# Adding each token's two expert rows on TensorE instead of on ScalarE and VectorE

## The chip, the cores and the metric

The kernel runs on one core of one Trainium2 chip. The metric is the device time of one execution in microseconds (us), the median of several runs. Five engines have instruction streams of their own: TensorE (PE), VectorE (DVE), ScalarE (ACT), GpSimd (POOL) and SyncE (SP, which here only waits and issues transfers). They meet through semaphores, which are called by their names in the code (`y_back`, `over_sum`, `x_done`).

## The reference

One step of a two-layer backbone, for 128 context tokens and 256 latent tokens (384 in all, width 1024, float32). Layer 0 has a Hyena and grouped-query attention mixer, layer 1 multi-head latent attention (MLA). Both layers end in a mixture of experts, and only its end matters here:

```python
    scores = sigmoid(x @ router_w)                   # 16 experts, the best group, the best two in it
    wsel = wsel / sum(wsel)                          # two gates for each token
    mid = silu(a) * up * gates[:, :, None]
    y = einsum('tef,efd->td', mid, w_down)           # each token: gate0 * row of expert 0 + gate1 * row of expert 1
    ...
    h = _rmsnorm(x, norm_ffn[l]) * (1.0 + sc2) + sh2
    x = x + g2 * _moe(h, ...)                        # g2: a vector over the 1024 columns, one for each group of tokens
```

After layer 0 the next layer begins with a norm of x; after layer 1 x is the output.

## The kernel before

The 384 tokens stand in three tiles (t = 0, 1, 2) of 128 partitions; `x[:, t, :]` is the residual stream. An expert stage (`experts(l)` on every engine, called from `moe(l)`) gathers token rows, runs the 16 experts in blocks of 64 rows on TensorE, and scatters each block's rows, not yet gated, into a DRAM table `y_rows` of 768 rows: row i is token i's first choice, row 384 + i its second. Rows that don't fit into an expert's 64 places go into further "over" blocks, in a loop on all engines (`over_block`). The last over block isn't scattered: TensorE adds its rows straight to their tokens with a table of zeros and gates (`token_table`).

What stands behind the loop in each layer is called the tail here:

- SP (`rows_back`, L770 to 776) and ACT (L1909 to 1912) wait for the last scatter (`over_stored`) and read `y_rows` back, tile by tile: ACT the first choices into `y_of[0]` (which is `xn`), SP the second choices into `y_of[1]`. Each transfer is 128 rows of 4 KB, one to a partition (512 KB). Both count on `y_back[t]`; a tile has landed when it stands at 32 more than before.
- ACT multiplies a tile's first rows by their gates (`scale_first`, L1915 to 1917).
- DVE multiplies the last over block by the vector g2 (L2595 to 2596, table `gate_halves`), PE turns it into token rows with `token_table` (L1393 to 1397, six products of 64 rows) in two PSUM banks for each tile, and counts `over_sum`.
- DVE joins a tile in `join(l, t, part)`: part 0 adds the second rows times their gates (L2605), part 1 multiplies by g2 (L2607), part 2 adds the result to x (L2609) and then the two PSUM banks (L2614), and counts `x_done`.

After layer 0, ACT and DVE norm each tile (`next_norm`, `norm_mean`, `norm_scale`) between the joins. PE runs 14 products on constants, which nobody reads, then `mixer_turn(1, 0)` (transposes of tile 0), ACT and nobody else modulates the transposed tile 0 (eight instructions of L1774), and PE projects it (`latent_in(0)`). ACT's order is: norm of tile 0, norm of tile 1, modulation of tile 0, norm of tile 2. SP waits for all of `y_back` before it sends the weights of `latent_in`, and for `over_sum` of all tiles before it sends the MLA projection weights; POOL waits for `over_sum` of all tiles before it loads nine small tables of MLA (`in_mla`). After layer 1, SP stores each tile of x when it is done (L824), and the program ends.

The order of every engine's work is that in which the code is written.

Of the kernel before, what the change touches and what calls it, by code (L numbers as in the profile page):

```python
# [193 lines left out]
def build_step(nc, d, o):  # L194
# [180 lines left out]
    with ExitStack() as ctx:  # L375
# [42 lines left out]
        gates_read = ck[:, 96:96 + 2 * NT].rearrange("p (t m) -> p t m", m=2)  # L418
# [120 lines left out]
        y_of = [xn, view(7680, NT, D)]  # L539
# [6 lines left out]
        gate_halves, token_ids, token_table = view(5120, 2, HY), view(6464, T), view(6848, T)  # L546
# [62 lines left out]
        y_scaled = sem("y_scaled")  # L609
# [84 lines left out]
        def _(sp):  # L694
# [134 lines left out]
        def _(pool):  # L829
# [45 lines left out]
            for l in range(2):  # L875
# [60 lines left out]
                pool.wait_ge(over_stored[l], nb * 16)  # L936
                pool.tensor_tensor(pool_mark[:, 2:3], pool_mark[:, 3:4], pool_mark[:, 3:4], ALU.mult)
# [36 lines left out]
        def _(pe):  # L974
# [254 lines left out]
            def experts(l):  # L1229
# [412 lines left out]
            for _ in range(14):  # L1642
# [69 lines left out]
        def _(act):  # L1712
# [133 lines left out]
            def experts(l):  # L1846
# [64 lines left out]
                for t in range(NT):  # L1911
                    act.dma_start(y_of[0][:, t, :], y_rows[P * t:P * t + P, :]).then_inc(y_back[t], 16)
                act.wait_ge(over_gathered[l], nb * 16 + 32)
# [127 lines left out]
            scale_first(0, 0)  # L2041
            scale_first(0, 1)
            next_norm(0)
            scale_first(0, 2)
# [45 lines left out]
            for t in range(NT):  # L2090
                scale_first(1, t)
# [3 lines left out]
        def _(dve):  # L2095
# [411 lines left out]
            def over_lists(l):  # L2507
# [4 lines left out]
                dve.tensor_copy(place_gate[:, :, 1], ps[MT_BANKS[0]][:, 256 + 2 * NOVER:256 + 3 * NOVER])  # L2512
                dve.drain().then_inc(over_rows, 1)
                dve.tensor_copy(row_now[:, :], rows_over[:, 1:2]).then_inc(row_ready[l], 1)

            def over_scales(l):
# [5 lines left out]
                for half in range(2):  # L2522
                    rows = slice(HALF * half, HALF * half + HALF)
                    dve.tensor_copy(gate_halves[rows, :, :], gb[rows, :, HY * half:HY * half + HY])

            def experts(l):
# [68 lines left out]
                for g in range(2):  # L2595
                    ins = dve.tensor_tensor(ysb[:, 1, HY * g:HY * g + HY], ps[Y_BANKS[0]][:, :], gate_halves[:, g, :], ALU.mult)
                ins.then_inc(over_done[l], 1)

            def join(l, t, part):
                ya, yb = y_of[0][:, t, :], y_of[1][:, t, :]  # L2600
                settle()
                if part == 0:
                    dve.wait_ge(y_back[t], 32 * (l + 1))
                    dve.wait_ge(y_scaled, NT * l + t + 1)
                    dve.scalar_tensor_tensor(out=ya, in0=yb, scalar=gates_read[:, t, 1:2], in1=ya, op0=ALU.mult, op1=ALU.add)  # L2605
                elif part == 1:
                    dve.tensor_tensor(ya, ya, gb[:, GRP[t], :], ALU.mult)  # L2607
                else:
                    dve.tensor_tensor(x[:, t, :], x[:, t, :], ya, ALU.add)  # L2609
                    dve.wait_ge(over_sum, NT * l + t + 1)  # L2610
                    settle()
                    for half in range(2):
                        part_of = x[:, t, HY * half:HY * half + HY]
                        ins = dve.tensor_tensor(part_of, part_of, ps[SUM_BANKS[t][half]][:, :], ALU.add)  # L2614
                    ins.then_inc(x_done, 1)
# [207 lines left out]
            for part in range(3):  # L2823
# [5 lines left out]
            join(0, 1, 2)  # L2829
# [4 lines left out]
            join(0, 2, 2)  # L2834
# [29 lines left out]
            for t in range(NT):  # L2864
                for part in range(3):
# [21 lines left out]
```

## Time and profile before

| | us |
|---|---|
| median of 3 runs | 871.5 (865.86 to 874.1) |
| the profiled execution, its own time | 869.39 |
| its span, first to last instruction | 867.5 |
| PE busy | 789.1 (91%) |
| DVE busy | 374.6 (43%) |
| ACT busy | 283.6 (33%) |
| POOL busy | 107.2 (12%) |
| HBM traffic over the span | 269 GB/s |
| mean granted TensorE clock | 0.968 of full |

How to read it: PE is busy nearly everywhere, and the chain that ended last runs 58% of the span through PE. The places where PE stands idle are the first microseconds and the two tails, after 457 us and after 844 us of the span. Busy shares over the whole span say nothing on a tail; for that the timeline of the tail is read, row by row. In the rows below, "x12" is the number of instructions in a row (a float32 product is shown as two), a bracket is the idle time of the engine ahead of the row and what ended it, PEld is the weight load, and SPq, ACTq are instructions that issue a transfer.

### The profile page before, as it was taken

What the parts mean: (1) busy time and instruction counts of PE and PEld (TensorE: products, weight loads), DVE (VectorE), ACT (ScalarE), POOL (GpSimd) and SP (SyncE); (2) the same over time, 40 slices, a digit from 0 to 9 for tenths busy, and PEclk for the clock granted to TensorE, in tenths of its full rate; (3) what the DMA queues carried; (4) which work ended last, traced back from release to release, by engine and by line L of the source; (5) the groups of instructions that cost most, each with busy time, mean ns of one, the idle gap of its engine ahead of it and who ended that gap; (6) DMA issues with size and microseconds to landing.
All of it is one profiled execution on the core that took longest, in us unless ns stands there. A gap on an engine that the chain in (4) does not pass through costs nothing.

```text
span 867.5 us, 12012 instructions
## 1 busy us (share of the span) xinstructions
PE 789.1 (91%) x4271; PEld 450.8 (52%) x4271; DVE 374.6 (43%) x875; ACT 283.6 (33%) x661; POOL 107.2 (12%) x153
## 2 busy tenths in 40 slices
PE   7889999999899999999974989999999999999870
PEld 4358755535444666555433546655544575555430
DVE  5670543543562443422226365475632434331126
ACT  1651222201540341222223347767610522222211
POOL 1400000010000011111122020330300111111120
PEclk9999999999999979999997999999999989999995
DMA  8993323699953387999988973220156679999974
GB/s 277 371 344 115 103 98 102 239 342 299 328 223 121 104 297 292 411 412 409 410 304 317 335 274 116 99 96 4 52 160 276 205 261 387 406 410 409 383 250 180
DMA packets 84088, 221.64 MB, mean 256 GB/s; under 512 B 9630, under 2 KB 19495, under 8 KB 83646
## 3 DMA queue, kind: packets, MB, share of 16 engines
q1 hardware_dynamic: 74174, 201.03, 63.6%
q0 software_dynamic: 8352, 16.30, 5.5%
q10 hardware_dynamic: 1504, 3.56, 1.1%
q8 instruction: 35, 0.57, 0.3%
q14 instruction: 23, 0.18, 0.1%
HBM read 216.28 MB, written 17.45 MB: 269 GB/s over the span
## 4 chain that ended last, share of the span: by engine, by line
PE 58%; issue 11%; DMA 10%; SPq 7%; DVE 7%; ACT 3%; POOLq 3%; DVEq 1%; POOL 1%; ACTq 0%
PE ps L998 53%; DMA arena<-in_moe_w_up_dram 4%; PE ps L1005 3%; SPq L739 2%; SPq L699 2%; PE ps L1240 2%; SPq L682 2%; DMA x<-in_x_sample_dram 2%; DVEq L2098 1%; POOLq L966 1%; DMA h_rows<-hT_xn 1%; DVE hT_xn L2605 1%; DMA hT_xn<-h_rows,row_now 1%; DVE x L2609 1%; DVE hT_xn L2607 1%
## 5 line engine op out<-in xcount | busy, mean ns | idle before, releaser
L998 PE MATMUL ps<-arena 128*64 128x256 f32 (+13 forms) x1244 | 230.7, 423 | 18.6 <-DMA arena<-in_moe_w_up_dram 7.9
L998 PEld LDWEIGHTS ps<-arena 128*64 128x64 f32 (+3 forms) x1244 | 125.0, 157 | 105.3 <-issue 58.4
L998 PE MATMUL ps<-ring,hT_xn 128*128 128x512 f32 (+2 forms) x384 | 133.3, 508 | 5.9 <-issue 5.3
L998 PEld LDWEIGHTS ps<-ring,hT_xn 128*128 128x128 f32 x384 | 73.2, 192 | 63.9 <-issue 59.5
L998 PE MATMUL ps<-ring,arena 128*64 128x256 f32 (+1 forms) x592 | 84.9, 435 | 1.3 <-ACT arena L1855 1.2
L1725 ACT ACTIVATE arena<-ps 128x256 f32<-128x256 f32 (+4 forms) x94 | 42.3, 463 | 86.8 <-PE ps L998 84.7
L998 PE MATMUL ps<-hT_xn,ring 128*128 128x384 f32 x192 | 62.1, 486 | 0.0
L2532 DVE TENSOR_TENSOR arena<-arena,ps 128x128 f32<-128x128 f32 x37 | 10.7, 288 | 116.2 <-ACT arena L1852 109.3
L998 PE MATMUL ps<-hT_xn,arena 128*64 128x256 f32 (+3 forms) x340 | 58.2, 428 | 1.9 <-DVE hT_xn L2194 1.7
L998 PEld LDWEIGHTS ps<-ring,arena 128*64 128x64 f32 x592 | 40.6, 137 | 36.6 <-issue 20.1
L1005 PE MATMUL ps<-ident,arena 128*128 128x128 f32 (+2 forms) x332 | 48.6, 280 | 7.6 <-DVE arena L2850 1.4
L998 PE MATMUL ps<-ring,condT 128*32 128x512 f32 x384 | 50.1, 648 | 2.7 <-DMA ring<-in_w_mod_dram 2.6
L1005 PEld LDWEIGHTS ps<-ident,arena 128*128 128x128 f32 (+2 forms) x332 | 36.8, 136 | 27.8 <-issue 14.3
L998 PEld LDWEIGHTS ps<-hT_xn,ring 128*128 128x128 f32 x192 | 36.5, 190 | 25.2
L998 PEld LDWEIGHTS ps<-hT_xn,arena 128*64 128x64 f32 (+1 forms) x340 | 27.7, 143 | 28.9 <-issue 23.1
L2535 DVE COPY arena<-ps 64x512 f32<-64x512 f32 x35 | 24.3, 694 | 39.5 <-PE ps L998 34.5
L1858 ACT ACTIVATE arena<-ps 64x512 f32<-64x512 f32 x35 | 20.7, 590 | 58.1 <-PE ps L998 46.9
L1852 ACT ACTIVATE arena<-ps 128x128 f32<-128x128 f32 x37 | 10.3, 278 | 86.1 <-PE ps L998 84.5
L1766 ACT ACTIVATE hT_xn<-x 128x1024 f32<-128x1024 f32 x12 | 12.7, 1055 | 68.0 <-DVE x L2329 54.2
L2166 DVE TENSOR_REDUCE negmax<-ps 128x1 f32<-128x384 f32 (+1 forms) x48 | 20.7, 463 | 26.6 <-PE ps L998 26.1
L2327 DVE TENSOR_TENSOR arena<-ps,gb 128x512 f32<-128x512 f32 x12 | 8.3, 691 | 50.0 <-PE ps L998 50.0
L1774 ACT ACTIVATE hT_xn<-ps,modT,modA 128x128 f32<-128x128 f32 x52 | 19.1, 465 | 29.9 <-PE ps L1005 28.9
(320 smaller groups left out, 895.2 us busy)
## 6 DMA issues: line engine op xcount, KB each, us to landing
ring<-in_w_mod_dram SPq DMA_DIRECT2D x48, 1024.0 KB, 8.4
arena<-in_moe_w_gate_dram SPq DMA_DIRECT2D x38, 512.0 KB, 10.3
arena<-in_moe_w_up_dram SPq DMA_DIRECT2D x38, 512.0 KB, 11.8
ring<-in_moe_w_down_dram SPq DMA_DIRECT2D x18, 1024.0 KB, 19.3
ring<-in_moe_w_gate_dram SPq DMA_DIRECT2D x28, 512.0 KB, 6.0
ring<-in_moe_w_up_dram SPq DMA_DIRECT2D x28, 512.0 KB, 8.3
arena<-in_moe_w_down_dram SPq DMA_DIRECT2D x20, 512.0 KB, 15.9
ring<-in_ev_w_in_dram SPq DMA_DIRECT2D x9, 1024.0 KB, 16.0
```

The lines of the kernel that those rows point to most:

```text
L682: eng.dma_start(dst, src).then_inc(s, 16)
L699: sp.dma_start(ring_view(i, shape, off)[rows], src).then_inc(piece_full[i % RING], 16)
L739: sp.dma_start(dst, src).then_inc(landed, 16)
L998: mm = pe.matmul(out, lhsT, rhs, **kw)
L1005: mm = pe.transpose(out, src, ident[:, :])
L1240: mm = pe.transpose(ps[XT_BANKS[half]][:, q * P:(q + 1) * P], src[:, (4 * half + q) * P:(4 * half + q + 1) * P], ident[:, :])
L1725: drain_inc(act.activation(dst, src, kw.pop("func", ACT.Copy), **kw), stage, i)
L1766: act.activation(xn[:, t, :], x[:, t, :], ACT.Square, accum_out=ssq[:, s, t:t + 1]).then_inc(squares, 1)
L1774: ins = act.activation(hT[:, k, t * P:(t + 1) * P], bank[:, j * P:(j + 1) * P], ACT.Identity, bias=modT[:, l, SH2 if which else SH1, k, GR ...
L1858: act.activation(dst, ps[Y_BANKS[e % 2]][0:HALF, :], ACT.Copy).then_inc(done[l], 1)
L2166: dve.tensor_reduce(negmax[:, c:c + 1], bank[:, 0:nk], AXX, ALU.max, negate=True).then_inc(negmax_ready, 1)
L2535: dve.tensor_copy(dst, ps[Y_BANKS[e % 2]][HALF:P, :]).then_inc(y_read[1][l], 1)
```

## The change

- `y_rows` is read back in another layout, `y_pairs` (128 partitions x tile x 2 x 1024): partitions 0 to 63 hold first choices (ACT's transfers), partitions 64 to 127 second choices (SP's); partition p of a half holds the rows of tokens p and 64 + p of the tile. Each transfer still moves 128 rows of 4 KB.
- A table `pair_table` (six tables of 128 x 64, one for each tile and u = 0, 1) holds a token's two gates on two diagonals. For each tile PE multiplies `pair_table` by `y_pairs`: four products of 128 rows, 64 output partitions and 512 columns, added to the banks that `token_table`'s products have begun. `over_sum` is counted after these. The gates of the other half's tokens come through a small product with `ident` in the expert stage (PE), four small copies (`over_lists`) and two instructions for the table (`over_scales`) on DVE.
- ACT's `scale_first` goes. The last over block is copied, not multiplied by g2. `join` has two parts: the PSUM banks times g2 into `xn`, and the addition to x.
- 8 instead of 14 idle products on PE ahead of layer 1's first transposes. The wait for the last gather (`over_gathered`) moves to POOL, and stays on ACT in layer 0 alone.

```diff
@@ rows_back on SP, and the same on ACT with y_pairs[0:HALF]
-                    sp.dma_start(y_of[1][:, t, :], y_rows[T + P * t:T + P * t + P, :]).then_inc(y_back[t], 16)
+                    sp.dma_start(y_pairs[HALF:P, t, :, :], y_rows[T + P * t:T + P * t + P, :].rearrange("(u p) n -> p u n", p=HALF)).then_inc(y_back[t], 16)
@@ TensorE
+                            mm = product(bank[HALF * half:HALF * half + HALF, 296:296 + 2 * NT], ident[:, HALF - HALF * half:P - HALF * half], ck[:, 96:96 + 2 * NT], start=True, stop=True)
...
                 for t in range(NT):
                     for half in range(2):
                         rows = slice(HALF * half, HALF * half + HALF)
-                        mm = product(ps[SUM_BANKS[t][half]][:, :], token_table[rows, P * t:P * t + P], ysb[rows, 1, HY * GRP[t]:HY * GRP[t] + HY], start=True, stop=True)
+                        product(ps[SUM_BANKS[t][half]][:, :], token_table[rows, P * t:P * t + P], ysb[rows, 1, 0:HY], start=True, stop=False)
+                for t in range(NT):
+                    pe.wait_ge(y_back[t], 32 * (l + 1))
+                    for half in range(2):
+                        for u in range(2):
+                            mm = product(ps[SUM_BANKS[t][half]][HALF * u:HALF * u + HALF, :], pair_table[:, 2 * t + u, :], y_pairs[:, t, u, HY * half:HY * half + HY],
+                                         start=False, stop=True)
                     mm.then_inc(over_sum, 1)
...
-            for _ in range(14):
+            for _ in range(8):
@@ ScalarE
-            def scale_first(l, t):
-                act.wait_ge(y_back[t], 32 * (l + 1))
-                act.activation(y_of[0][:, t, :], y_of[0][:, t, :], ACT.Copy, scale=gates_read[:, t, 0:1]).then_inc(y_scaled, 1)
@@ VectorE: over_lists, over_scales, experts, join
+                turned = ps[MT_BANKS[0]][:, 296:296 + 2 * NT].rearrange("p (t m) -> p t m", m=2)
+                for k, own, rows in ((0, 0, slice(0, HALF)), (1, 1, slice(HALF, P))):
+                    dve.tensor_copy(gates_pair[rows, :, own], gates_read[rows, :, k])
+                    dve.tensor_copy(gates_pair[rows, :, 1 - own], turned[rows, :, k])
...
-                for half in range(2):
-                    rows = slice(HALF * half, HALF * half + HALF)
-                    dve.tensor_copy(gate_halves[rows, :, :], gb[rows, :, HY * half:HY * half + HY])
+                dve.tensor_tensor(twice, ident[:, 0:HALF], ident[:, HALF:P], ALU.add)
+                settle()
+                dve.tensor_tensor(pair_table, every(twice, 2 * NT, HALF), gates_pair.rearrange("p t u -> p (t u)").unsqueeze(2).broadcast_to([P, 2 * NT, HALF]), ALU.mult)
...
-                for g in range(2):
-                    ins = dve.tensor_tensor(ysb[:, 1, HY * g:HY * g + HY], ps[Y_BANKS[0]][:, :], gate_halves[:, g, :], ALU.mult)
-                ins.then_inc(over_done[l], 1)
+                dve.tensor_copy(ysb[:, 1, 0:HY], ps[Y_BANKS[0]][:, :]).then_inc(over_done[l], 1)
...
                 if part == 0:
-                    dve.wait_ge(y_back[t], 32 * (l + 1))
-                    dve.wait_ge(y_scaled, NT * l + t + 1)
-                    dve.scalar_tensor_tensor(out=ya, in0=yb, scalar=gates_read[:, t, 1:2], in1=ya, op0=ALU.mult, op1=ALU.add)
-                elif part == 1:
-                    dve.tensor_tensor(ya, ya, gb[:, GRP[t], :], ALU.mult)
+                    dve.wait_ge(over_sum, NT * l + t + 1)
+                    for half in range(2):
+                        cols = slice(HY * half, HY * half + HY)
+                        dve.tensor_tensor(xn[:, t, cols], ps[SUM_BANKS[t][half]][:, :], gb[:, GRP[t], cols], ALU.mult)
                 else:
-                    dve.tensor_tensor(x[:, t, :], x[:, t, :], ya, ALU.add)
-                    dve.wait_ge(over_sum, NT * l + t + 1)
                     settle()
-                    for half in range(2):
-                        part_of = x[:, t, HY * half:HY * half + HY]
-                        ins = dve.tensor_tensor(part_of, part_of, ps[SUM_BANKS[t][half]][:, :], ALU.add)
-                    ins.then_inc(x_done, 1)
+                    dve.tensor_tensor(x[:, t, :], x[:, t, :], xn[:, t, :], ALU.add).then_inc(x_done, 1)
```

In the program's order DVE's tail of layer 0 reads before (a row is an instruction form with the partitions and elements of its output; xn is the second half of the buffer hT_xn):

```order
390 L2596 TENSOR_TENSOR arena<-ps,arena 128x512 x2
391 L2605 SCALAR_TENSOR_TENSOR hT_xn<-arena,ck,hT_xn 128x1024
392 L2607 TENSOR_TENSOR hT_xn<-hT_xn,gb 128x1024
393 L2609 TENSOR_TENSOR x<-x,hT_xn 128x1024
394 L2614 TENSOR_TENSOR x<-x,ps 128x512 x2
395 L2605 SCALAR_TENSOR_TENSOR hT_xn<-arena,ck,hT_xn 128x1024
396 L2144 TENSOR_SCALAR ssq<-ssq 128x1
397 L2607 TENSOR_TENSOR hT_xn<-hT_xn,gb 128x1024
398 L2149 RECIPROCAL ssq<-ssq 128x1
399 L2151 TENSOR_SCALAR hT_xn<-x,ssq 128x1024
400 L2609 TENSOR_TENSOR x<-x,hT_xn 128x1024
401 L2614 TENSOR_TENSOR x<-x,ps 128x512 x2
```

and after the change:

```order
393 L2600 COPY arena<-ps 128x512
394 L2607 TENSOR_TENSOR hT_xn<-ps,gb 128x512 x2
395 L2610 TENSOR_TENSOR x<-x,hT_xn 128x1024
396 L2607 TENSOR_TENSOR hT_xn<-ps,gb 128x512 x2
397 L2145 TENSOR_SCALAR ssq<-ssq 128x1
398 L2610 TENSOR_TENSOR x<-x,hT_xn 128x1024
399 L2150 RECIPROCAL ssq<-ssq 128x1
400 L2152 TENSOR_SCALAR hT_xn<-x,ssq 128x1024
401 L2607 TENSOR_TENSOR hT_xn<-ps,gb 128x512 x2
```

Each tile loses two instructions of 1024 columns on DVE, and the norm of tile 0 (RECIPROCAL, TENSOR_SCALAR) now stands behind the whole join of tile 1, where it stood ahead of tile 1's addition to x.

On PE the tail of layer 0 reads before:

```order
200 L998 MATMUL ps<-arena 128x512 x6
201 L998 MATMUL ps<-rowsel,ident 128x256 x14
202 L1005 MATMUL ps<-ident,hT_xn 128x128 x8
203 L998 MATMUL ps<-ring,hT_xn 128x416 x8
204 L1005 MATMUL ps<-ident,hT_xn 128x128 x16
```

and after the change (twelve products with `pair_table` come between the six of `token_table` and the idle ones; layer 1's tail ends with the same twelve):

```order
203 L1000 MATMUL ps<-arena 128x512 x6
204 L1000 MATMUL ps<-arena 64x512 x12
205 L1000 MATMUL ps<-rowsel,ident 128x256 x8
206 L1007 MATMUL ps<-ident,hT_xn 128x128 x8
207 L1000 MATMUL ps<-ring,hT_xn 128x416 x8
```

PE's idle products and the transposes of tile 0 now stand behind the products of tile 2, which wait for the last rows that are read back.

## Rows read from the trace of the kernel before

**Rows 1.** Timeline of layer 1's tail: start us, us, engine, line, operation, forms.

```profile
840.51 1.94 PE L998 MATMUL ps<-arena 128*64 128x512 f32 x8 [1.28 <-DMA arena<-in_moe_w_down_dram]
...
842.10 1.29 SPq L776 DMA_DIRECT2D arena<-y_rows  x3
842.10 1.32 ACTq L1912 DMA_DIRECT2D hT_xn<-y_rows  x3
842.49 1.29 DVE L2596 TENSOR_TENSOR arena<-ps,arena 128x512 f32<-128x512 f32 x2 [2.16 <-PE ps L998]
...
843.92 2.85 PE L998 MATMUL ps<-arena 64*128 64x512 f32 x12 [1.47 <-DVE arena L2596]
...
847.12 1.15 ACT L1917 ACTIVATE hT_xn<-hT_xn,ck 128x1024 f32<-128x1024 f32 x1 [7.58 <-DMA hT_xn<-y_rows]
848.38 1.28 DVE L2605 SCALAR_TENSOR_TENSOR hT_xn<-arena,ck,hT_xn 128x1024 f32<-128x1024 f32 x1 [4.60 <-ACT hT_xn L1917]
...
849.88 1.15 ACT L1917 ACTIVATE hT_xn<-hT_xn,ck 128x1024 f32<-128x1024 f32 x1 [1.61 <-DMA hT_xn<-y_rows]
851.04 1.23 DVE L2609 TENSOR_TENSOR x<-x,hT_xn 128x1024 f32<-128x1024 f32 x1
852.09 1.15 ACT L1917 ACTIVATE hT_xn<-hT_xn,ck 128x1024 f32<-128x1024 f32 x1 [1.06 <-DMA hT_xn<-y_rows]
852.34 1.28 DVE L2614 TENSOR_TENSOR x<-x,ps 128x512 f32<-128x512 f32 x2
853.65 11.14 SPq L824 DMA_DIRECT2D out_dram<-x  x3
...
863.15 1.29 DVE L2614 TENSOR_TENSOR x<-x,ps 128x512 f32<-128x512 f32 x2
```

**Rows 2.** Timeline of layer 0's tail and the start of layer 1.

```profile
454.64 2.85 PE L998 MATMUL ps<-arena 64*128 64x512 f32 x12 [1.48 <-DVE arena L2596]
...
457.41 6.31 PE L998 MATMUL ps<-rowsel,ident 128*128 128x256 f32 x28
...
466.09 0.62 POOL L682 DMA_DIRECT2D arena<-in_rope_m_dram  x1
466.41 1.06 ACT L1766 ACTIVATE hT_xn<-x 128x1024 f32<-128x1024 f32 x1 [4.35 <-DVE x L2614]
...
469.35 0.75 DVE L2151 TENSOR_SCALAR hT_xn<-x,ssq 128x1024 f32<-128x1024 f32 x1
...
470.16 1.97 PE L1005 MATMUL ps<-ident,hT_xn 128*128 128x128 f32 x8 [6.44 <-DVE hT_xn L2151]
...
474.44 2.89 ACT L1774 ACTIVATE hT_xn<-ps,modT,modA 128x128 f32<-128x128 f32 x8
...
477.42 7.34 PE L998 MATMUL ps<-ring,hT_xn 128*128 128x416 f32 x16 [5.29 <-issue]
...
487.16 11.41 PE L998 MATMUL ps<-ring,hT_xn 128*128 128x416 f32 x32 [0.61 <-ACT hT_xn L1774]
```

**Rows 3.** ACT's reads of y_rows in layer 0's tail: issue times, times to landing.

```profile
L1912 ACTq DMA_DIRECT2D hT_xn<-y_rows x3: 392/445/594, 451.2 to 452.1; - x3
...
DMA to landing us min/median/max: 4.9/7.2/8.9
```

**Rows 4.** Stretches: length; busy of PE, PEld, DVE, ACT, POOL; PEclk, DMA share, GB/s.

```profile
220.00:226.00 6.00, 4.88 (x25) 3.36 (x24) 0.53 (x3) 3.19 (x6) 0.68 (x1) 1.00 1.08 211
466.00:467.00 1.00, 0.00 (x0) 0.00 (x0) 0.84 (x2) 0.59 (x1) 0.70 (x2) 0.92 1.01 416
844.00:851.00 7.00, 2.77 (x12) 1.11 (x12) 2.51 (x2) 2.26 (x2) 0.00 (x0) 0.87 1.01 412
```

**Rows 5.** Transfers by name: issues, KB of one, median us from issue to landing.

```profile
ring<-in_ev_w_out_dram SPq DMA_DIRECT2D x4, 512.0 KB
...
arena<-in_rope_m_dram POOLq DMA_DIRECT2D x1, 64.0 KB, 8.8
```

**Rows 6.** Groups by form: count, busy us, mean ns of one, idle before.

```profile
L998 PE MATMUL ps<-arena 128*64 128x33 f32 x48 | 2.7, 223 | 0.0
```

More of the change, by code:

```diff
@@ L417, in build_step @@
         place_gate, last_place = ck[:, 64:64 + 2 * NOVER].rearrange("p (c k) -> p c k", k=2), ck[:, 18:20]
-        gates_read = ck[:, 96:96 + 2 * NT].rearrange("p (t m) -> p t m", m=2)
+        gates_read, gates_pair = (ck[:, a:a + 2 * NT].rearrange("p (t m) -> p t m", m=2) for a in (96, 104))
         ids = ck[:, 32:32 + 4 * NT].rearrange("p (k i) -> p k i", k=2)
@@ L538, in build_step @@
         htok = xn
-        y_of = [xn, view(7680, NT, D)]
+        y_pairs = view(7680, NT, 2, D)
         spare = flat_hT.rearrange("p (a b) -> p a b", b=D)
@@ L545, in build_step @@
         first_pair = view(7232, NT, P)
-        gate_halves, token_ids, token_table = view(5120, 2, HY), view(6464, T), view(6848, T)
+        twice, pair_table = view(5120, HALF), view(5184, 2 * NT, HALF)
+        token_ids, token_table = view(6464, T), view(6848, T)
         other_row = {"start": hT[:, :, :].rearrange("p a b -> p (a b)")[:, 0:512], "gqa": view(6144, 512),
@@ L608, in build_step @@
         y_back = [sem(f"y_back{t}") for t in range(NT)]
-        y_scaled = sem("y_scaled")
         latent_squares, latent_sums, lora_root, lora_ready = sem("latent_squares"), sem("latent_sums"), sem("lora_root"), sem("lora_ready")
@@ L936, in _ @@
                 pool.wait_ge(over_stored[l], nb * 16)
+                pool.tensor_tensor(pool_mark[:, 1:2], pool_mark[:, 3:4], pool_mark[:, 3:4], ALU.mult)
+                pool.wait_ge(over_gathered[l], nb * 16 + 32)
                 pool.tensor_tensor(pool_mark[:, 2:3], pool_mark[:, 3:4], pool_mark[:, 3:4], ALU.mult)
@@ L1911, in experts @@
                 for t in range(NT):
-                    act.dma_start(y_of[0][:, t, :], y_rows[P * t:P * t + P, :]).then_inc(y_back[t], 16)
-                act.wait_ge(over_gathered[l], nb * 16 + 32)
-            def scale_first(l, t):
-                act.wait_ge(y_back[t], 32 * (l + 1))
-                act.activation(y_of[0][:, t, :], y_of[0][:, t, :], ACT.Copy, scale=gates_read[:, t, 0:1]).then_inc(y_scaled, 1)
+                    act.dma_start(y_pairs[0:HALF, t, :, :], y_rows[P * t:P * t + P, :].rearrange("(u p) n -> p u n", p=HALF)).then_inc(y_back[t], 16)
+                if l == 0:
+                    act.wait_ge(over_gathered[l], nb * 16 + 32)
             def next_norm(t):
@@ L2040, in _ @@
             preload(ACT.Sqrt)
-            scale_first(0, 0)
-            scale_first(0, 1)
             next_norm(0)
-            scale_first(0, 2)
             next_norm(1)
@@ L2089, in _ @@
             moe(1)
-            for t in range(NT):
-                scale_first(1, t)
         @block.vector
@@ L2594, in experts @@
                 dve.wait_ge(y_stored[1][l], 16 * (NPAIR // 2))
-                for g in range(2):
-                    ins = dve.tensor_tensor(ysb[:, 1, HY * g:HY * g + HY], ps[Y_BANKS[0]][:, :], gate_halves[:, g, :], ALU.mult)
-                ins.then_inc(over_done[l], 1)
+                dve.tensor_copy(ysb[:, 1, 0:HY], ps[Y_BANKS[0]][:, :]).then_inc(over_done[l], 1)
             def join(l, t, part):
-                ya, yb = y_of[0][:, t, :], y_of[1][:, t, :]
-                settle()
                 if part == 0:
-                    dve.wait_ge(y_back[t], 32 * (l + 1))
-                    dve.wait_ge(y_scaled, NT * l + t + 1)
-                    dve.scalar_tensor_tensor(out=ya, in0=yb, scalar=gates_read[:, t, 1:2], in1=ya, op0=ALU.mult, op1=ALU.add)
-                elif part == 1:
-                    dve.tensor_tensor(ya, ya, gb[:, GRP[t], :], ALU.mult)
-                else:
-                    dve.tensor_tensor(x[:, t, :], x[:, t, :], ya, ALU.add)
-                    dve.wait_ge(over_sum, NT * l + t + 1)
+                    dve.wait_ge(over_sum, NT * l + t + 1)
+                    for half in range(2):
+                        cols = slice(HY * half, HY * half + HY)
+                        dve.tensor_tensor(xn[:, t, cols], ps[SUM_BANKS[t][half]][:, :], gb[:, GRP[t], cols], ALU.mult)
+                else:
                     settle()
-                    for half in range(2):
-                        part_of = x[:, t, HY * half:HY * half + HY]
-                        ins = dve.tensor_tensor(part_of, part_of, ps[SUM_BANKS[t][half]][:, :], ALU.add)
-                    ins.then_inc(x_done, 1)
+                    dve.tensor_tensor(x[:, t, :], x[:, t, :], xn[:, t, :], ALU.add).then_inc(x_done, 1)
             def moe(l):
@@ L2820, in _ @@
             moe(0)
-            for part in range(3):
+            for part in range(2):
                 join(0, 0, part)
@@ L2828, in _ @@
             norm_scale(2, 0)
-            join(0, 1, 2)
             join(0, 2, 0)
@@ L2833, in _ @@
             norm_scale(2, 1)
-            join(0, 2, 2)
             norm_tile(2, 2)
@@ L2864, in _ @@
             for t in range(NT):
-                for part in range(3):
+                for part in range(2):
                     join(1, t, part)
```

## The prediction

> **What bounds the kernel now.** I read three views in this order: the chain of waits, which leads through PE nearly everywhere and leaves it only in the two tails; the timeline of each tail; and the stretches with the moved bytes, since both tails begin with a read-back. A shorter tail after layer 0 starts everything behind it earlier, because MLA and the second expert stage hang on PE's order; a shorter tail after layer 1 ends the program earlier. So each tail counts in full.
>
> In layer 1's tail both queues issue the read-back at 842.1, and ACT's three gate products start at 847.12, 849.88 and 852.09, each just as its tile lands [rows 1]. DVE then needs four steps for a tile, of 1.28, about as much for the product with g2, 1.23 and 1.28. It starts at 848.38 and ends at 863.15 + 1.29 = 864.44, so it is 5.4 us for each tile and lags the last landing by 12 us. DVE is the bound. PE did its six products by 846.8 and is idle [rows 1]. The last store ends 3 us later.
>
> In layer 0's tail the landings are 451.2 + 4.9 = 456.1, about 451.7 + 7.2 = 458.9, and 452.1 + 8.9 = 461.0 [rows 3]. The same DVE work stands behind them: x of tile 0 is done at 466.4, its norm is written at 469.35 + 0.75 = 470.1, PE turns it, ACT modulates it from 474.44 for 2.89, and `latent_in(0)` starts at 477.42 [rows 2]. That start is where I measure the gain of this tail.
>
> **The change part by part, layer 1's tail.** New work on PE: four products for each tile, 128 rows into 64 output partitions and 512 columns. The down product of the expert stage has this shape exactly, and its four take 1.94 us [rows 1]. Two that write different output halves run side by side in it (eight records of 0.6 in 1.94), and the new ones are written in pairs of this kind too. New work on DVE for a tile: two reads of a PSUM bank with one SBUF operand, as L2614 does, 1.29 for both, 0.1 for the drain, and the addition to x at 1.23 [rows 1]: 2.6 in place of 5.4. ACT's 1.15 goes.
>
> With the landings as they are, tile 0 is on PE from 847.1 to 849.05, and DVE is done with it at 851.7. Tile 1 is on PE from 849.9 to 851.85, DVE done at 854.5. Tile 2 is on PE from 852.1 to 854.05; DVE is free at 854.5, and done at 857.2. Against 864.4 that is **7.2 us earlier**. Each store of 512 KB is issued as its tile ends, 2.7 apart, so the last has 3 us behind it as now.
>
> **Layer 0's tail.** The last over block is copied in one instruction where two took 1.29, so PE's six products start 0.6 earlier, 454.0 instead of 454.64, and end at 456.9 [rows 1, 2]. Pair products: tile 0 456.9 to 458.85, tile 1 to 460.85, tile 2 from its landing at 461.0 to 462.95. DVE: tile 0 done at 458.85 + 2.6 = 461.5, g2 of tile 1 at 462.8, tile 1 done at 464.3, norm of tile 0 written at 465.4, g2 of tile 2 at 466.7, mean of tile 1 at 466.9, root on ACT at 467.2. On PE 28 records of the idle products took 6.31 [rows 2], so 16 of them take 3.6 and end at 466.55; only then do the transposes of tile 0 run (1.97 at half clock [rows 2], 1.1 at full), and their first bank is there at 467.1. ACT modulates from 467.2 to 470.1. `latent_in(0)` starts at 470.1 instead of 477.42: **7.3 us earlier**. In short it starts 9.1 us after the last tile has landed.
>
> The clock: PE went idle at 463.7 and the granted clock fell in the stretch 466 to 467 [rows 2, 4], so `latent_in(0)` began at half clock and took 7.34 for 16 records, where the next two tiles took 11.41 for 32, or 5.7 for one [rows 2]. After the change the idle time ahead of it is 2.5 us. The clock may stay, which gives 1.6, or fall, which gives nothing; I take **0.8**.
>
> What is waited for longer: `over_sum` of all tiles now comes at 463.0, so POOL's nine MLA tables are issued about 2 us later. The last is issued at 466.09 and needs 8.8 [rows 2, 5], so it lands at 475 now and at 477 then; it is first wanted behind `latent_in` of tiles 1 and 2, which end no sooner than 489. SP's projection weights wait the same 2 us and are used later still. If this cover were gone, the price would be those 2 us.
>
> **The expert stages.** PE gets two small products with two records each: the 48 records of 33 columns took 2.7 us, 56 ns each [rows 6], so 0.2 for each layer. PE has no idle time there, so I count **-0.4** for both. DVE gets four tiny copies and loses two large ones, and it is busy for 43% of the span: nothing as long as it waits for the others there, and at most 0.6 if the copies delayed one expert.
>
> Sum: 7.2 + 7.3 + 0.8 - 0.4 = 14.9 us off, if the read-back lands as it does now.
>
> **The read-back itself** is what no row shows. It moves 3 MB at 412 GB/s [rows 4]. Now a transfer fills 128 partitions; then ACT's fills 64 and SP's the other 64. The nearest row is the four transfers of 512 KB from `ev_w_out` [rows 5], each into 64 partitions and all on one queue: there the DMA engines are as busy (1.08) and move only 211 GB/s [rows 4]. So a half of the partitions alone takes half the rate. Here two queues feed both halves at once. If the engines serve them in turn and don't meet, the rate stays at 412; if they meet at one half all the time, the 7.7 us of transfer become about 15.
>
> The Trainium skill, "SBUF — State Buffer", Door 1, says that partitions 0 to 63 reach 8 of the 16 ports, and "DMA: Bandwidth & Descriptors", Rules for kernel authors, advises against two transfers to disjoint halves of the partitions, since they share the engines, and asks for one of 128. The row of 211 GB/s agrees with the first; no row shows two queues on two halves. By the second read strictly there would be no loss against one transfer, by the first at its worst the sum would be near zero.
>
> With D the delay of the last landing, layer 0 loses D and layer 1 loses D - 0.4 (DVE is free that much after PE). The gain is 14.9 + 0.4 - 2 D for D above 0.4. Both queues start together and alternate; I take D = 0.9, near the full-rate end, since the queues do share every engine tile by tile now and stay within a fraction of a us of each other. Gain 13.5. The profiled execution took 869.4, which gives 855.9. It lies 2.1 below the median and inside the spread of 865.9 to 874.1, so I put the median at **856.5**.
>
> **The rivals.**
> - *Both halves fill (forecast).* D from 0 to 1.5, gain 12 to 15, 854 to 858 with the spread. Chance 0.48.
> - *The halves partly meet.* D from 1.5 to 6, gain 12 down to 3, 858 to 867. For it: an engine that has begun a row to one half holds it while another writes the same half, and a tile counts as landed when the slowest of 16 engines is done. Against: two queues can go on in turn. Chance 0.28.
> - *Half rate.* D = 7.7, gain near 0: layer 1's last tile lands at 859.8 and ends at 864.3 as now, layer 0 likewise. 868 to 872. Chance 0.17. For it the row of 211 GB/s, against it that only one half was fed there.
> - *Slower.* The same mechanism with the queues also in each other's way: from D = 7.7 on every us costs two. To be over 1% slower (880) it takes D = 12, 3 MB in 20 us or 160 GB/s, below anything that the half-partition stretch shows (211). Chance 0.03.
> - *Layer 0's gain goes.* Weights or tables come too late behind `latent_in`; then 6.5 of layer 1 stay, 864. The 12 us of slack speak against it. Chance 0.04.
>
> **How the numbers follow.** About 1% (8.7 us) is what a measurement of this kernel can tell from no change. A gain over 8.7 needs D below 3.3: nearly all of the first case and half of the second, 0.47 + 0.15, and 0.01 from the rest: 0.63. Slower by over 1%: 0.03. Within 1%: 0.34. The range 852 to 867 holds the first two cases and the last and leaves out 0.2, the half rate and the slower one.
>
> **What would show it.** In the profile after: the reads of `y_rows` to land after 4.9, 7.2 and 8.9 us as now, or later (D is read there directly), and the GB/s of the stretch 844 to 851, then shifted by 8, near 410 or near 210; the pair products at 1.94 for eight records; 2.6 us of DVE for a tile in layer 1's tail; `latent_in(0)` 9.1 us behind the last landing and at full clock or not; the last store issued some 5 us after the last landing, where it was 12. The prediction is wrong if the read-back gets slower, if the pair products don't run side by side (3.4 for a tile, and 1.5 us lost in each tail), or if the tables of MLA are waited for.

## The result, and the profile after

| | before | after |
|---|---|---|
| median of 20 runs, us | 871.5 (864.7 to 875.6) | 865.2 (859.8 to 870.4) |
| ratio after / before | | 0.9932 [0.991, 0.9954] |
| the profiled execution, its own time | 869.4 | 859.8 |
| its span | 867.5 | 857.9 |
| mean granted TensorE clock | 0.968 | 0.981 |

The change gives 5.9 us (4.0 to 7.8), 0.7%, where my median of 856.5 stood for 15. The profiled execution of after lies 5.4 us below its median, that of before 2.1 below its own, so the two spans flatter the change: tails are compared below from the issue of the read-back on, and not as positions in the span.

The engines' busy time moved as the diff says: in part 1 of the page of after PE has 9 us more than before, DVE 16 less, ACT 7 less.

```profile
PE 798.2 (93%) x4315; PEld 451.5 (53%) x4315; DVE 358.2 (42%) x869; ACT 276.6 (32%) x655; POOL 108.4 (13%) x155
```

The chain that ended last has a new entry, by line on the page: the read-back itself, with 3% of the span.

```profile
PE ps L1000 56%; DMA arena<-in_moe_w_up_dram 4%; PE ps L1007 3%; DMA arena<-y_rows 3%; SPq L739 3%; SPq L699 2%; PE ps L1242 2%; SPq L682 2%; DMA x<-in_x_sample_dram 2%; POOLq L968 1%; DVEq L2099 1%; PE ps L1258 1%; POOLq L964 1%; ACT hT_xn L1783 1%; DMA mod_rows<-modrow 1%
```

The timeline of layer 1's tail (start us, us, engine, line, operation, forms, in brackets the idle time ahead and what ended it), which answers to [rows 1]:

```profile
834.76 1.90 SPq L776 DMA_DIRECT2D arena<-y_rows  x3
834.76 2.28 ACTq L1921 DMA_DIRECT2D arena<-y_rows  x3
834.91 0.69 DVE L2600 COPY arena<-ps 128x512 f32<-128x512 f32 x1 [1.15 <-PE ps L1000]
...
842.69 3.52 PE L1000 MATMUL ps<-arena 128*64 128x512 f32 x8 [4.10 <-DMA arena<-y_rows]
846.26 1.29 DVE L2607 TENSOR_TENSOR hT_xn<-ps,gb 128x512 f32<-128x512 f32 x2 [10.66 <-PE ps L1000]
846.97 1.94 PE L1000 MATMUL ps<-arena 128*64 128x512 f32 x8 [0.76 <-DMA arena<-y_rows]
...
848.88 6.39 SPq L824 DMA_DIRECT2D out_dram<-x  x3
...
850.33 1.94 PE L1000 MATMUL ps<-arena 128*64 128x512 f32 x8 [1.43 <-DMA arena<-y_rows]
...
852.32 1.29 DVE L2607 TENSOR_TENSOR hT_xn<-ps,gb 128x512 f32<-128x512 f32 x2 [0.78 <-PE ps L1000]
853.68 1.22 DVE L2610 TENSOR_TENSOR x<-x,hT_xn 128x1024 f32<-128x1024 f32 x1
```

Each group of eight product records starts as its tile lands, and PE and DVE wait for the transfers; before, the transfers were in and DVE was the bound. Tile 2 is there at 850.33, which is 15.6 us after the first issue; before it was there at 852.09 - 842.10 = 10.0 us after it [rows 1]. DVE ends at 853.68 + 1.22 = 854.90, or 20.1 us after the issue, where it was 22.3.

The transfers in that tail, by the view of one tensor on ACT and then on SP (durations of the issue, first and last issue, us from issue to landing). ACT's took 4.9, 7.2 and 8.9 in layer 0's tail before [rows 3]:

```profile
L1921 ACTq DMA_DIRECT2D arena<-y_rows x3: 652/730/842, 834.8 to 836.3; - x3
...
DMA to landing us min/median/max: 7.9/11.5/14.0
```

```profile
L776 SPq DMA_DIRECT2D arena<-y_rows x3: 596/602/609, 834.8 to 836.0; - x3
...
DMA to landing us min/median/max: 5.5/10.5/13.7
```

Two stretches (length; busy of PE, PEld, DVE, ACT, POOL; granted clock, DMA share, GB/s):

```profile
837.00:849.00 12.00, 7.05 (x24) 1.70 (x20) 2.56 (x4) 0.00 (x0) 0.00 (x0) 0.86 1.03 254
842.00:846.00 4.00, 3.31 (x8) 0.77 (x8) 0.00 (x0) 0.00 (x0) 0.00 (x0) 0.57 1.06 275
```

The DMA engines are as busy as before (1.03 against 1.01) and move 254 GB/s in place of 412 [rows 4]. The second row is the clock: PE had been idle for 4.1 us, and over the stretch in which it ran tile 0's products the granted clock was 0.57, so it was at the lower of its two levels (1.2 GHz, half) for most of it.

The timeline of layer 0's tail, which answers to [rows 2]; the first issue is at 447.79:

```profile
447.79 1.93 SPq L776 DMA_DIRECT2D arena<-y_rows  x3
...
455.73 2.67 PE L1000 MATMUL ps<-arena 128*64 128x512 f32 x8 [2.21 <-DMA arena<-y_rows]
...
463.28 0.41 PEld L1000 LDWEIGHTS ps<-arena 128*64 128x64 f32 x4 [1.30 <-DMA arena<-y_rows]
...
465.36 3.72 PE L1000 MATMUL ps<-rowsel,ident 128*128 128x256 f32 x16
...
468.92 1.05 PE L1007 MATMUL ps<-ident,hT_xn 128*128 128x128 f32 x8
...
472.62 7.52 PE L1000 MATMUL ps<-ring,hT_xn 128*128 128x416 f32 x16 [2.65 <-issue]
```

The weight load at 463.28 is the landing of tile 2, 15.5 us after the issue (before 461.0 - 450.92 = 10.1). `latent_in(0)` starts 24.8 us after the issue, where it was 477.42 - 450.92 = 26.5.

### The profile page after: what moved, and what is told of

It reads as the page before. It is cut to its first block, busy times and chain, and to the rows that moved or that the text cites. A ratio compares the mean times of both kernels' runs of the same rounds, so it can differ in the third digit from the quotient of the medians.

```text
span 857.9 us, 12068 instructions
## 1 busy us (share of the span) xinstructions
PE 798.2 (93%) x4315; PEld 451.5 (53%) x4315; DVE 358.2 (42%) x869; ACT 276.6 (32%) x655; POOL 108.4 (13%) x155
## 4 chain that ended last, share of the span: by engine, by line
PE 62%; issue 11%; DMA 9%; SPq 7%; DVE 4%; ACT 2%; POOLq 2%; DVEq 1%; POOL 1%; ACTq 0%
PE ps L1000 56%; DMA arena<-in_moe_w_up_dram 4%; PE ps L1007 3%; DMA arena<-y_rows 3%; SPq L739 3%; SPq L699 2%; PE ps L1242 2%; SPq L682 2%; DMA x<-in_x_sample_dram 2%; POOLq L968 1%; DVEq L2099 1%; PE ps L1258 1%; POOLq L964 1%; ACT hT_xn L1783 1%; DMA mod_rows<-modrow 1%
## 5 line engine op out<-in xcount | busy, mean ns | idle before, releaser
L1000 PE MATMUL ps<-arena 128*64 128x256 f32 (+12 forms) x1292 | 245.1, 435 | 24.9 <-DMA arena<-y_rows 10.1
L1000 PEld LDWEIGHTS ps<-arena 128*64 128x64 f32 (+3 forms) x1292 | 128.5, 157 | 122.9 <-issue 60.2
L1007 PEld LDWEIGHTS ps<-ident,arena 128*128 128x128 f32 (+2 forms) x332 | 36.6, 135 | 27.3 <-issue 13.8
L2167 DVE TENSOR_REDUCE negmax<-ps 128x1 f32<-128x384 f32 (+1 forms) x48 | 20.8, 463 | 24.8 <-PE ps L1000 24.3
```

What stands on the lines that cost most here:

```text
L1000: mm = pe.matmul(out, lhsT, rhs, **kw)
L1007: mm = pe.transpose(out, src, ident[:, :])
L2167: dve.tensor_reduce(negmax[:, c:c + 1], bank[:, 0:nk], AXX, ALU.max, negate=True).then_inc(negmax_ready, 1)
```

## The experiments

Two theories stand against each other for the 15.5 us. **Which partitions**: a transfer whose partitions are all in 0 to 63 (or all in 64 to 127) is held to about half the rate, and two queues on the two halves don't make up for it. **The rest of the form**: 64 partitions as such, two rows for each partition, the order in which rows are read from DRAM, or something else in the changed kernel.

### e1: the same sum, transfers of 128 partitions

`y_rows` is laid out anew, so that 128 consecutive rows of the table are what the 128 partitions want for one u. Only the constant table of row numbers and the two transfers change.

```diff
-    c["ids"] = np.concatenate([token, token, token, token + T], 1)
+    p, t = np.arange(P)[:, None], np.arange(NT)[None, :]
+    place = [2 * P * t + P * (p // HALF) + HALF * m + p % HALF - NO_ROW for m in range(2)]
+    c["ids"] = np.concatenate([token, token, place[0], place[1]], 1)
...
-                    sp.dma_start(y_pairs[HALF:P, t, :, :], y_rows[T + P * t:T + P * t + P, :].rearrange("(u p) n -> p u n", p=HALF)).then_inc(y_back[t], 16)
+                    sp.dma_start(y_pairs[:, t, 1, :], y_rows[2 * P * t + P:2 * P * t + 2 * P, :]).then_inc(y_back[t], 16)
...
-                    act.dma_start(y_pairs[0:HALF, t, :, :], y_rows[P * t:P * t + P, :].rearrange("(u p) n -> p u n", p=HALF)).then_inc(y_back[t], 16)
+                    act.dma_start(y_pairs[:, t, 0, :], y_rows[2 * P * t:2 * P * t + P, :]).then_inc(y_back[t], 16)
```

> The changed kernel, with the rows of y_rows in another order (a constant table): for each tile and u, the 64 first choices and the 64 second choices of the same tokens stand one behind the other. So each of the six read-backs fills 128 partitions with 128 consecutive rows again, and y_pairs and everything behind it are as in the changed kernel. Theory H (what was lost is the two queues that each write one half of the partitions): the last tile lands 10 us after the issue instead of 15.5, each tail is 5 to 5.6 us shorter, the kernel is about 10 us faster than the changed one, ratio to before 0.980 to 0.985. Rival S (the loss comes from the pair products, their wait, or from the read-back standing next to PE's work): the landings stay at 15.5 us and the time at that of the changed kernel, 0.993.

Measured: 854.2 us (850.9 to 856.3) against 872.0 on the same chip, ratio 0.9797 [0.9758, 0.9836], 17.7 us off (14.3 to 21.1). ACT's transfers in layer 1's tail, then the stretch while they run:

```profile
L1923 ACTq DMA_DIRECT2D arena<-y_rows x3: 361/446/452, 835.5 to 836.4; - x3
...
DMA to landing us min/median/max: 5.0/7.3/9.3
```

```profile
838.00:845.00 7.00, 5.57 (x26) 1.64 (x22) 2.32 (x3) 0.00 (x0) 0.33 (x2) 1.00 1.01 406
```

And the ends of both tails in its timeline:

```profile
472.34 7.36 PE L1002 MATMUL ps<-ring,hT_xn 128*128 128x416 f32 x16 [2.66 <-issue]
...
835.52 1.29 SPq L778 DMA_DIRECT2D arena<-y_rows  x3
...
849.14 1.23 DVE L2612 TENSOR_TENSOR x<-x,hT_xn 128x1024 f32<-128x1024 f32 x1
```

The read-back is back at 406 GB/s and lands as before. Layer 1's tail ends 850.37 - 835.52 = 14.85 us after its issue, 7.5 less than before; layer 0's issue is at 453.06, so `latent_in(0)` starts 19.3 after it, 7.2 less. What the change lacked is in its transfers; with these put right, both tails gain what the forecast said of them (7.2 and 7.3).

### e2: the kernel before, with transfers to halves

The other direction: the old sum is kept whole, and only the form of the transfers is taken over.

```diff
-        y_of = [xn, view(7680, NT, D)]
+        y_both = view(7680, NT, 2, D)
+        y_of = [y_both[:, :, 0, :], y_both[:, :, 1, :]]
...
-                    sp.dma_start(y_of[1][:, t, :], y_rows[T + P * t:T + P * t + P, :]).then_inc(y_back[t], 16)
+                    sp.dma_start(y_both[HALF:P, t, :, :], y_rows.rearrange("(k r) n -> r k n", k=2)[P * t + HALF:P * t + P, :, :]).then_inc(y_back[t], 16)
...
-                    act.dma_start(y_of[0][:, t, :], y_rows[P * t:P * t + P, :]).then_inc(y_back[t], 16)
+                    act.dma_start(y_both[0:HALF, t, :, :], y_rows.rearrange("(k r) n -> r k n", k=2)[P * t:P * t + HALF, :, :]).then_inc(y_back[t], 16)
```

> The kernel before, with the read-back alone changed: ACT's transfer of a tile fills partitions 0 to 63 with the first and second choices of 64 tokens, SP's fills 64 to 127. Same bytes, same number of transfers, same work on all engines; first choices stand in the arena instead of xn. Theory H: the last landing comes at 15.5 us instead of 10 after the issue. DVE starts 3 us later (first landing at 7.9 instead of 4.9) and is the bound behind it, 5.4 us for a tile against 3 us between landings, so each tail is longer by 3 us: 6 us slower in all, ratio 1.007. If D counted in full in both tails, 11 us, 1.013. Rival S: no difference.

Measured: 877.2 us against 872.0, ratio 1.0064 [1.0034, 1.0094]. The stretch of its read-back:

```profile
848.00:859.00 11.00, 2.15 (x11) 0.70 (x7) 4.66 (x5) 2.29 (x2) 0.18 (x1) 0.76 1.04 255
```

```profile
845.19 1.90 SPq L777 DMA_DIRECT2D arena<-y_rows  x3
...
852.86 1.15 ACT L1918 ACTIVATE arena<-arena,ck 128x1024 f32<-128x1024 f32 x1 [9.02 <-DMA arena<-y_rows]
...
868.89 1.29 DVE L2615 TENSOR_TENSOR x<-x,ps 128x512 f32<-128x512 f32 x2
```

The rate is the same 255 GB/s with the old products, so the form of the transfers is enough to cause it. The price is small in layer 1's tail, because DVE hides the late landings of tiles 1 and 2: it waits for tile 0 alone, which lands 7.7 us after the issue and not 5.0, and the tail gets 25.0 us long in place of 22.3. In layer 0's tail `latent_in(0)` starts 31.0 us after the issue and not 26.5, which is 4.5 more and not the 3 that I expected. There another transfer sets the start: ACT stands still until the last gather of token rows (`over_gathered`) is in, though tile 0 has landed. In the kernel before and in e2:

```profile
459.78 0.20 ACT L1763 ACTIVATE act_mark<-act_mark 1x1 f32<-1x1 f32 x1 [5.72 <-DMA hT_xn<-h_rows,row_now]
```

```profile
461.96 0.20 ACT L1764 ACTIVATE act_mark<-act_mark 1x1 f32<-1x1 f32 x1 [9.60 <-DMA hT_xn<-h_rows,row_now]
```

The gather is issued about 1 us behind the read-back and took 7.6 us to land before and 12.2 in e2, so ACT goes on 8.9 and 13.3 us after the read-back's issue: these are the 4.5 us. In after, too, the gather took 12.0 us, but there only ACT's norm of tile 0 waits for it (to 460.86), and tile 0 is done at 461.03. Both tails together are 7.2 us longer, and the ratio gives 5.6 (3.0 to 8.2). The last tile lands 5.2 us later here, nearly as in after (5.6); the slow sum hides half of that in layer 1's tail, where after, against e1, shows nearly all (20.1 - 14.85 = 5.3).

### e3 and e4: the same number of partitions in two places

Both start from e1's layout and read only 64 of the 128 partitions back, so each transfer is 256 KB with one row for each partition. The other half of the expert rows is left out of the read-back, so these two don't compute the step, and only times are read. They differ in one number.

```diff
-                    sp.dma_start(y_pairs[:, t, 1, :], y_rows[2 * P * t + P:2 * P * t + 2 * P, :]).then_inc(y_back[t], 16)
+                    sp.dma_start(y_pairs[32:96, t, 1, :], y_rows[2 * P * t + P + 32:2 * P * t + P + 96, :]).then_inc(y_back[t], 16)
...
-                    act.dma_start(y_pairs[:, t, 0, :], y_rows[2 * P * t:2 * P * t + P, :]).then_inc(y_back[t], 16)
+                    act.dma_start(y_pairs[32:96, t, 0, :], y_rows[2 * P * t + 32:2 * P * t + 96, :]).then_inc(y_back[t], 16)
```

e4 has 0:64 in place of 32:96.

> Leaves out half of the read-back: with the row order of e1_full_rows, each of the six transfers moves only 64 rows of 4 KB, into partitions 32 to 95 (so the other rows are not added rightly; only times are read). Theory P (it matters which 64 partitions: 32 to 63 and 64 to 95 lie in different halves): full rate, 1.5 MB at about 400 GB/s, the last landing about 6 us after the issue. Rival C (any transfer to 64 partitions is slow): about 10 us, the same as in e4_window_0_64.

> Leaves out half of the read-back like e3_window_32_96, same bytes and number of rows, but both queues write partitions 0 to 63. Theory P: half the rate, 1.5 MB at about 205 GB/s, the last landing about 10 us after the issue, 4 us later than in e3_window_32_96. Rival C: no difference between the two.

Measured, ACT's transfers, the stretch of e3 (partitions 32 to 95) and its fastest 2 us:

```profile
L1923 ACTq DMA_DIRECT2D arena<-y_rows x3: 566/615/847, 830.7 to 832.2; - x3
...
DMA to landing us min/median/max: 3.8/4.5/5.3
```

```profile
832.00:836.00 4.00, 3.78 (x18) 1.66 (x20) 0.07 (x1) 0.00 (x0) 0.33 (x2) 1.00 0.99 336
833.00:835.00 2.00, 2.00 (x11) 0.68 (x7) 0.00 (x0) 0.00 (x0) 0.33 (x2) 1.00 0.99 391
```

and of e4 (partitions 0 to 63):

```profile
L1923 ACTq DMA_DIRECT2D arena<-y_rows x3: 520/619/850, 828.9 to 830.3; - x3
...
DMA to landing us min/median/max: 4.7/7.2/8.5
```

```profile
831.00:838.00 7.00, 5.46 (x27) 1.69 (x24) 2.34 (x3) 0.00 (x0) 0.33 (x2) 1.00 0.96 193
```

The same bytes, rows, queues and number of partitions: the last lands 6.8 us after the first issue in 32 to 95 and 9.9 in 0 to 63, with 336 and 193 GB/s on the way. Sixty-four partitions as such aren't slow; sixty-four in one half are. The total times, 849.4 and 848.6 us, are one run each and can't tell the two apart. The Trainium skill, "SBUF — State Buffer", Door 1, states that partitions 0 to 63 reach 8 of the 16 ports and 64 to 127 the other 8. It follows that a window from 32 to 95 reaches all. These two runs agree with it.

### e5: one queue for both halves

```diff
+                    sp.dma_start(y_pairs[0:HALF, t, :, :], y_rows[P * t:P * t + P, :].rearrange("(u p) n -> p u n", p=HALF)).then_inc(y_back[t], 16)
                     sp.dma_start(y_pairs[HALF:P, t, :, :], y_rows[T + P * t:T + P * t + P, :].rearrange("(u p) n -> p u n", p=HALF)).then_inc(y_back[t], 16)
...
-                    act.dma_start(y_pairs[0:HALF, t, :, :], y_rows[P * t:P * t + P, :].rearrange("(u p) n -> p u n", p=HALF)).then_inc(y_back[t], 16)
```

> The changed kernel with all six read-backs on SP's queue: for each tile the first choices into partitions 0 to 63, then the second choices into 64 to 127. Theory P (a half of the partitions takes half the rate, whatever feeds it): the engines write one half at a time, 3.1 MB at about 210 GB/s plus 2 us to the first byte, the last landing 17 us after the first issue; that it took 15.5 with two queues would then be all that the second queue brings. Rival Q (two queues get in each other's way, and one alone is fast): the last landing at 10 to 12 us.

Measured, in one run: 865.2 us against 870.8, which lies inside the spread of after (859.8 to 870.4). The stretch:

```profile
841.00:854.00 13.00, 6.91 (x26) 1.81 (x22) 2.51 (x3) 0.00 (x0) 0.33 (x2) 0.89 1.04 216
```

Issued from 838.5 to 841.7, the last lands 17.2 us after the first issue; the halves follow each other at 216 GB/s, near the 211 of the one-half stretch in the kernel before [rows 4]. So one after the other costs 17.2 us and two queues 15.6: feeding both halves at once, which I had counted on, brings 1.6 us of the 7 that were to be had.

### e9: the new order of rows, transfers to halves

e1 changed two things, the form of the transfers and where a row stands in DRAM. This one has e1's order and after's halves.

```diff
-                    sp.dma_start(y_pairs[:, t, 1, :], y_rows[2 * P * t + P:2 * P * t + 2 * P, :]).then_inc(y_back[t], 16)
+                    sp.dma_start(y_pairs[HALF:P, t, :, :], y_rows[2 * P * t:2 * P * t + 2 * P, :].rearrange("(u p) n -> p u n", p=P)[HALF:P, :, :]).then_inc(y_back[t], 16)
...
-                    act.dma_start(y_pairs[:, t, 0, :], y_rows[2 * P * t:2 * P * t + P, :]).then_inc(y_back[t], 16)
+                    act.dma_start(y_pairs[0:HALF, t, :, :], y_rows[2 * P * t:2 * P * t + 2 * P, :].rearrange("(u p) n -> p u n", p=P)[0:HALF, :, :]).then_inc(y_back[t], 16)
```

> The rows of y_rows in the order of e1_full_rows, but each transfer fills 64 partitions with two rows each, as in the changed kernel: ACT's partitions 0 to 63, SP's 64 to 127. It takes the two edits of e1_full_rows apart. Theory P: the last landing at 15.5 us after the issue, as in the changed kernel. Rival O (the order of the rows in DRAM made e1_full_rows fast): 10 us.

Measured, ACT's transfers:

```profile
L1923 ACTq DMA_DIRECT2D arena<-y_rows x3: 653/727/852, 837.1 to 838.7; - x3
...
DMA to landing us min/median/max: 7.8/10.9/13.3
```

The last lands at 838.7 + 13.3 = 852.0, 14.9 us after the first issue, near after's 15.6 and far from e1's 10.1. The order in DRAM may explain 0.7 us and not the 5.6. The time, 861.4 us in one run against 870.8, lies inside the spread of after as well.

### e7 and e6: the idle products and the clock

In the forecast the clock was a coin's throw. e7 gives after its 14 idle products back. e6 is e1 with three idle products ahead of tile 0's transposes and seven behind them, in a bank that is free there.

```diff
-            for _ in range(8):
+            for _ in range(14):
```

```diff
-            for _ in range(8):
+            for _ in range(3):
                 product(ps[XT_BANKS[1]][:, 0:2 * P], ident[:, :], rowsel[:, :, :].rearrange("p a b -> p (a b)"), start=True, stop=True)
             mixer_turn(1, 0)
+            for _ in range(7):
+                product(ps[3][:, 0:2 * P], ident[:, :], rowsel[:, :, :].rearrange("p a b -> p (a b)"), start=True, stop=True)
```

> The changed kernel with 14 idle products instead of 8, as before the change: undoes that part alone. Theory: in the changed kernel the transposes of tile 0 wait for the idle products (they end at 469.1, the norm is written at 467.3), so six more products (12 records, 2.7 us) start latent_in(0) 2.7 us later at the same clock: 2.7 us slower than the changed kernel, ratio 0.996. If the idle time that they fill keeps the clock up, latent_in(0) takes 1.6 less and the loss is 1 us, 0.994. Rival: no effect, since they only fill idle time.

> e1_full_rows, with PE's eight idle products ahead of layer 1's first transposes replaced by three ahead of them and seven behind them. In e1_full_rows the transposes of tile 0 begin at 468.65 right behind the idle products although the norm is written at 467.15, and latent_in(0) runs at half clock (7.36 us). Theory: PE idles for less than 2 us ahead of latent_in(0), the clock stays and it takes 5.7 us, 1.6 less; ACT can start 0.5 earlier. In all 2 us faster than e1_full_rows, ratio 0.977 to 0.978. Rival (the clock fell for another reason, or it comes back as fast anyway): as e1_full_rows, 0.980.

Measured: e7 867.3 us against 870.8, ratio 0.9945 [0.9915, 0.9975], not to be told from after's 0.9932. Its timeline, PE:

```profile
468.83 6.31 PE L1000 MATMUL ps<-rowsel,ident 128*128 128x256 f32 x28
...
478.68 5.82 PE L1000 MATMUL ps<-ring,hT_xn 128*128 128x416 f32 x16 [2.65 <-issue]
```

Behind the longer block the granted clock is 1.00 through the same idle time of 2.65 and all of `latent_in(0)`, which takes 5.82 and not 7.52 (in after the clock is 0.50 from 474 to 477); but it stands on the path, and `latent_in(0)` starts 27.3 us after the issue (451.36) and not 24.8. It loses 2.5 and wins 1.7.

e6: 851.6 us (849.6 to 853.9) against 870.8, ratio 0.9763 [0.973, 0.9797]. Its timeline, PE:

```profile
460.09 1.16 PE L1009 MATMUL ps<-ident,hT_xn 128*128 128x128 f32 x8 [0.57 <-DVE hT_xn L2156]
...
461.09 3.19 PE L1002 MATMUL ps<-rowsel,ident 128*128 128x256 f32 x14
...
464.42 5.83 PE L1002 MATMUL ps<-ring,hT_xn 128*128 128x416 f32 x16
```

Behind the transposes the idle products fill the time in which ACT modulates, so they cost nothing, and no idle time stands ahead of `latent_in(0)`: it starts 18.4 us after the issue (445.98), 0.8 sooner than in e1, and takes 5.83 in place of 7.36. The 2.4 us are read in this tail of the profile. In layer 1's tail of the same execution DVE ends 18.0 us after the issue, where it was 14.85 in e1: PE's last down product had waited for its weights and began only with the issue (826.75), and the granted clock was 0.50 from 830 to 834. So the spans of the two can't be compared. The two ratios differ by 0.0034 (3 us), but their intervals overlap, so the total is no proof of it. It is the fastest version here, 2.4% below the kernel before.

## Why the prediction was wrong on the size, point by point

- **The step that failed: D, the delay of the last landing.** I took 0.9, "near the full-rate end, since the queues do share every engine tile by tile now". It is 15.6 - 10.0 = 5.6 us in layer 1's tail and 15.5 - 10.1 = 5.4 in layer 0's. By my own formula the gain is then 14.9 + 0.4 - 2 x 5.5 = 4.3, and 5.9 (4.0 to 7.8) was measured. With the tails' terms alone it is 7.2 + 7.3 + 0.4 - 11 = 3.9, and the two tails gave 2.2 + 1.7 = 3.9. The row that I had, 211 GB/s for one half, was the right one to lean on; I set it aside for an argument that no row carried. This is the rival *the halves partly meet* near its far end (D from 1.5 to 6, 858 to 867), which had 0.28, and its outcome within 1% had 0.34 against 0.63.
- **From the sum to the median.** The sum gave 13.5 us off. I took it from the profiled execution of before, which lies 2.1 below the median, and added 0.6, so my median of 856.5 stands for 15.0 off 871.5. That put 1.5 us more into the forecast than its terms have.
- **Layer 1's tail, 7.2 us if the rows land as before.** Right: 7.5 in e1. With the delay as it is in after, 7.2 - (5.6 - 0.4) = 2.0, and 22.3 - 20.1 = 2.2 was there.
- **Layer 0's tail, 7.3 us, and `latent_in(0)` 9.1 us behind the last landing.** Right: 7.2 in e1; in after 472.62 - 463.28 = 9.3 behind the landing, and 26.5 - 24.8 = 1.7 in all. What I had not read in the rows of before is that ACT, and DVE behind it, waited there for the last gather until 459.78 and not for tile 0, which was in at 456.1 (e2). The sum is not touched by it, since it went by the times as they were.
- **The prices of instructions.** The product records of a tile took 1.94 at full clock, as the down product does. DVE needs 2.6 for a tile (852.32 to 854.90). The copy took 0.69 for 1.29. The one price that I had not foreseen is 3.52 for tile 0 in layer 1's tail and 2.67 in layer 0's, since PE had been idle and the clock had fallen (granted 0.57 and 0.73 in the stretches 842 to 846 and 455 to 459); in layer 0 tile 1 ran at 0.50 too (459 to 463). In layer 1 it costs nothing, because tile 1 lands at 846.97 and DVE is free soon after. In layer 0 it costs next to nothing, because PE takes up tile 2 when that lands.
- **The clock, 0.8 us.** Nothing: `latent_in(0)` took 7.52, before 7.34. The idle time ahead of it, 2.65, is what I had worked out (2.5). With eight idle products ahead of the transposes the clock fell, with 14 it stayed (e7).
- **MLA's tables and weights, no cost.** Held: `latent_in` of tiles 1 and 2 takes 11.41 in the timeline of after, as it did before [rows 2], and the transposes behind it come after the same 0.70 us of waiting for ACT in both.
- **The expert stages, 0.4 lost.** Not settled. The tails alone give 2.2 + 1.7 = 3.9 of after's 5.9, and 7.5 + 7.2 = 14.7 of e1's 17.7. So 2.0 and 3.0 are left over; 3.9 lies just outside the interval of after (4.0 to 7.8), 14.7 just inside that of e1 (14.3 to 21.1). One row fits a further gain: from the start of `latent_in(0)` to layer 1's first issue it is 364.7 us in before and 365.6 in e2, and 361.5 to 364.6 in the eight executions with the new sum (362.1 in after, 363.2 in e1). That is about 2 us, but the spread is as large, and no run takes that stretch apart.
- **The skill's two pages.** The rate in one half (193, 211 and 216 GB/s) agrees with the Trainium skill, "SBUF — State Buffer", Door 1, in every run here. The Trainium skill, "DMA: Bandwidth & Descriptors", Rules for kernel authors, says that two transfers to disjoint halves serialize, since they share the same engines, and asks for one of 128 partitions. I had read that as no loss against one transfer, and that was the wrong reading: halves that follow each other, each at the rate of a half, give e5's 216 GB/s. Two queues reached 254, near that and far from 412, so the runs bear the advice out.

What stays open is why two queues on two halves reach 254 GB/s and not 412, though all 16 engines serve both. One transfer of 512 KB after another on one queue lands every 2.46 us (12.3 us for five of them in e5), in after every 2.0 (10.1 for five). The forecast's reason for its second rival, an engine that holds a row to a busy half while the other half is idle, would do this, but no view here shows a single engine's order, so the reason stays a guess.

## What to carry to other kernels

When a bound is removed from a chain, read what the transfers ahead of it take in their new form, for they were hidden until then: here they took back 12 of 18 us (5.9 in after, 17.7 in e1). If a layout asks for rows in one half of the partitions, change the order in which they are written (a table of constants did it) so that each transfer fills all 128. Products that keep the clock belong where PE waits anyway, right ahead of the work that is to profit, and not ahead of the transposes on the path.

## What the runs showed of the hardware that I had not expected

- Two queues that each fill one half of the partitions move 254 and 255 GB/s (after, e2), one queue with both in turn 216, and 128 partitions 406 to 412, all with the DMA engines at a busy share of 1.01 to 1.04. That share doesn't tell a full rate from half of one; the GB/s do.
- The window of partitions 32 to 95 has no such limit: 336 GB/s over 4 us, and 391 in the middle two of them (e3).
- A gather issued about 1 us behind the read-back suffers with it: 7.6 and 7.7 us to landing behind transfers of 128 partitions (before, e1), 12.0 and 12.2 behind those to halves (after, e2).
- Issuing a transfer takes the queue's engine longer in the new form: 0.60 us on SP and 0.73 on ACT for 64 partitions with two rows each, 0.43 and 0.45 for 128 with one row (e1). It isn't the second row, for 64 partitions with one row each take 0.59 and 0.62 (e3, e4). The last issue is 0.6 us later by this in after; whether that adds to the 5.6 isn't shown.
